# Exchanging the halves of each weight chunk that VectorE and GpSimd turn into low parts

## The chip, the cores and the metric

The kernel runs on one core of a Trainium2 chip. The metric is the device time of one execution in microseconds (us), as the median of several runs. Engines are named as in the profile: PE is TensorE, PEld its weight loads, DVE is VectorE, ACT is ScalarE, POOL is GpSimd, SP is SyncE, which issues the loads of weights.

## The reference, cut to what matters

Two transformer-like blocks follow each other on 256 tokens (272 with 16 extra ones in the first block), with a model width of 1024, all in float32.

```
block 1: n = rmsnorm(h); z = n @ w_in          -> q, k, v, glu, two gates
         differential attention, causal depthwise conv (31 taps), gates
         h += m @ w_out
         up = conv3(rmsnorm(h) @ w_up); h += (silu(gate) * val) @ w_down     (hidden width 2816)
         h = rmsnorm(h)
block 2: z = rmsnorm(h) @ w_in_2               -> rope attention, HGRN2 recurrence, gates
         h += mixed @ w_out_2
         cross attention to 256 memory tokens (wq_x, wkv_x, wo_x)
         h += (silu(a) * b) @ w_down, with a, b = rmsnorm(h) @ w_up
out = rmsnorm(h)
```

The change touches none of these formulas. It concerns how the weight matrices are prepared for the matmuls.

## The kernel before

**Weights as chunks.** All weight matrices are laid out as 166 chunks of 128 partitions x 2048 columns (1 MB), in the order in which they are used. SP loads them into the slots of a ring in SBUF. One chunk gives two output tiles of 128 channels (eight blocks of 128 rows each, 24 matmuls a tile when the chunk is split).

**Split products.** Most phases keep float32 precision by splitting. A value is rounded to a high part (type fp32r), and the low part is the value minus the high part. A product is then three passes of fast matmuls: high weight x high input, high weight x low input, low weight x high input. So PE needs a chunk's high part when it begins the chunk, and its low part only for the third pass of its first tile (`wait_low`, which waits for both halves).

**Who makes the parts.** ACT makes the high part in two copies of 1024 columns, the columns of half 1 first and those of half 0 second (line L997). `split_high` counts these copies. The low part is made by `low_half` (L404), one subtraction of 128 x 1024 for each half:

```
def high_parts(phase, i, c, free):        # ScalarE, L997
    ...
    for half in (1, 0):
        cols = slice(half * HALF_CHUNK, (half + 1) * HALF_CHUNK)
        sc.activation(parts[:, p, cols], ring[:, slot, cols], ACT.Copy).then_inc(split_high, 1)

def low_half(eng, phase, i, c, half):     # L404
    ...
    eng.wait_ge(split_high, STREAM.split(phase, i, c) * 2 - half)
    eng.tensor_tensor(parts[:, LOW - HIGH + p, cols], ring[:, slot, cols], parts[:, p, cols].bitcast(F32), ALU.subtract)\
       .then_inc(split_low[half], 1)
```

So the wait of half 1 is met after the first copy, and that of half 0 after the second. Before the change DVE makes half 1 and POOL makes half 0 (`low_v`, `low_g`, and the call in `add_tiles`). In the phases heads1 and mem_v POOL makes both halves itself (`both`); the change leaves them as they are. The DVE halves that are concerned number 112. The parts are double buffered: ACT may write the high part of chunk c+2 when PE has finished chunk c, and SP may reload a ring slot when both halves of the low part are made.

**Order of the work.** Every engine runs a queue written out by hand, and the low halves stand at fixed places in the queues of DVE and POOL. The places that matter are these.

- up1 (the first block's gate and value projections, 5 loop iterations of two groups, and one group at the end, `up1_end`). A group is two chunks, that is four tiles e = 0 to 3. For each tile ACT makes a first tap (L974), DVE adds two taps (L1678, L1679, reading the tile in PSUM and an accumulator in SBUF), and for e = 2, 3 DVE multiplies by the silu of the gate (L1684, two inputs in SBUF). ACT computes the silus after e = 1, and then copies a chunk's high part; it copies the second chunk's after its tap of e = 3. DVE's queue for a group is: taps e0, taps e1, low half, taps e2, L1684, taps e3, L1684, low half. POOL's is: low half, low half, and then the high and low parts of the two hidden tiles (L2011, L2015).
- down1: nothing but chunks of the down projection, with one low half a chunk on each engine. DVE has the tables for rope in between (`tables1`, L1705 to L1729), then low halves again.
- heads2 (4 iterations, 8 chunks each): attention and the recurrence run beside the projections. POOL makes differences for the decays (L2081, L2082), ACT their exponentials (L1264), DVE the products `level` (L1769, L1771, two inputs in SBUF), and PE the products of these (L818, L828). Low halves stand in between.
- up2 and down2: as up1 and down1, without taps. DVE scales a tile by the norm (L1962, L1969) and multiplies by the silu (L1971).

Of the kernel before, what the change touches and what calls it, by code (L numbers as in the profile page):

```python
# [222 lines left out]
def blocks_kernel(nc, a):  # L223
    ctx = ExitStack()
    with ctx:
# [56 lines left out]
        def col(name, j=0, n=1):  # L282
            return table[:, AT[name] + j:AT[name] + j + n] if isinstance(j, int) else \
                table[:, bass.ds(j + AT[name], n)]
# [107 lines left out]
        def splits_between(phase, then):  # L392

            if phase in SPLIT:
                return [(phase, 2, 2, 3), (phase, 3, 4, 5), (then, 0, 6, 7), (then, 1, 8, 8)]
            return [(then, 0, 4, 5), (then, 1, 6, 7)] if then else []

        def low_half(eng, phase, i, c, half):

            slot, p = STREAM.at[phase][5][c % len(STREAM.at[phase][5])], STREAM.parity(phase, c)  # L400
# [5 lines that stand above are left out]
# [1042 lines left out]
        def _(ve):  # L1448
# [167 lines left out]
            def add_tiles(phase, dst, width, then=None, raw=None, low=None, weight=None, which=None):  # L1616

                def low_raw(t):
                    ve.wait_ge(x_high_ready, INPUTS[which] * KB + t + 1)
                    ve.scalar_tensor_tensor(low[:, t, 0:SEQ], dst(t), col(weight, t), raw[:, t, 0:SEQ].bitcast(F32),  # L1620
                                            ALU.mult, ALU.subtract).then_inc(x_low_ready, 1)

                for t in range(KB + 1):
                    if raw is not None and t == KB:
                        low_raw(t - 1)
                    for name, c, _, at in splits_between(phase, then):
                        if t == at:
                            low_half(ve, name, 0, c, 1)
                    if t < KB:
                        b = STREAM.bank(phase, t)  # L1630
                        ve.wait_ge(tile_done, STREAM.done(phase, 0, t))
                        ve.scalar_tensor_tensor(dst(t), ps[:, b, 0:width], HALF[phase], dst(t), ALU.mult, ALU.add)\  # L1632
                          .then_inc(tile_read[b], 1)
                    if raw is not None and 0 < t < KB:
                        low_raw(t - 1)
# [5 lines left out]

            HALF = {"mix_out1": 0.5, "mix_out2": 0.5, "cross_out": 1.0}
            def low_v(phase, i, c):
                low_half(ve, phase, i, c, 1)

            def down_low(down, between=None):
                for d in range(2, 8):
                    low_v(down, d // 4, d % 4)
                    if between and d == 3:
                        between()  # L1650
                for d in range(3):
                    low_v(down + "_end", 0, d)

            add_tiles("mix_out1", lambda t: res[:, t, Q0:T1], TQ, "up1")
            norm(TQ, lambda k: res[:, k, Q0:T1], lambda k: sq[:, k, 0:TQ], "norm_ffn_w", 3)
            x_low_parts(x_low, sq, x_high, TQ, "ffn1")

            def behind(phase, i, c, up):

                if phase == up:  # L1660
                    low_v(up, i, c + 2)
                else:
                    low_v("down" + up[-1], 0, c)
# [250 lines left out]
            for t in range(KB):  # L1914
# [8 lines left out]
                if t in (5, 7):  # L1923
                    low_v("mix_out2", 0, (t - 5) // 2)
            low_mixed(7)
            add_tiles("mix_out2", lambda t: res2[:, t, :], SEQ, "cross_q", cross_high, cross_low, "norm_x_g_2", "cross")
            inverse_root(SEQ, 6)
            n.next(bank_full[4], 3)
# [12 lines left out]
            for h in range(4):  # L1941
# [9 lines left out]
                if h < 2:  # L1951
                    query_x(h + 2)
            add_tiles("cross_out", lambda t: res2[:, t, :], SEQ, "up2", x_high, x_low, "norm_ffn_g_2", "ffn2")
            inverse_root(SEQ, 7)

# [32 lines left out]
        def _(gp):  # L1988
# [1 line left out]
            n = Tally("gpsimd")  # L1990

            def low_g(phase, i, c):
                low_half(gp, phase, i, c, 0)

            def add_squares(which, first, end, width):

# [21 lines left out]
            def ffn_parts(up, down, made, width):  # L2018

                add_squares("ffn" + up[-1], 1, 5, width)  # L2020
                low_g(up, 0, 0)
                add_squares("ffn" + up[-1], 5, 7, width)
                low_g(up, 0, 1)
                with gp.Fori(0, 5) as i:
                    n.enter(up, i)
                    for g in range(2):
                        low_g(up, i, 2 * g + 2)
                        low_g(up, i, 2 * g + 3)
                        made(up, i, g)
                        hidden_parts(i * 4 + 2 * g)  # L2030
                    n.leave(5)
                low_g(down, 0, 0)
                low_g(down, 0, 1)
                low_g(down, 0, 2)
                made(up + "_end", 0, 0)
                hidden_parts(20)
                for d in range(3, 8):
                    low_g(down, d // 4, d % 4)
                for d in range(3):
                    low_g(down + "_end", 0, d)  # L2040
# [151 lines left out]
```

## Time and profile before

| what | value |
| --- | --- |
| time, median of 3 runs | 1288.91 us (1288.39 to 1289.3) |
| the profiled execution: its own time | 1288.91 us |
| the profiled execution: span of the core | 1287.1 us |
| mean granted TensorE clock | 0.968 of full speed |
| PE busy | 1192.1 us, 93% |
| DVE busy | 701.5 us, 55% |
| ACT busy | 572.4 us, 44% |
| POOL busy | 570.1 us, 44% |

The times of rows are microseconds from the start of the span. A busy share is a mean over very different stages; what counts for a change is which engine's work ends last in the stage that it touches. "Idle before" in a row is the time that the engine had nothing to run ahead of it, with the instruction that ended the wait.

### The profile page before, as it was taken

The numbers are of one execution on the slowest core, as the hardware profiler recorded it, in microseconds if no ns is written. First come the engines' busy times: TensorE is split into PE (matmuls) and PEld (weight loads), VectorE is DVE, ScalarE is ACT, GpSimd is POOL, SyncE is SP. The second block draws the span as 40 slices with busy tenths as digits, with TensorE's granted clock in tenths as the row PEclk, the third lists the DMA queues.
The fourth block names the chain that finished last, engine by engine and source line by source line (L and its number), as shares of the span: only waits on it lengthen the run. The fifth ranks groups of instructions, "written<-read, shape, count | busy, mean of one in ns | idle before, by whom it ended". The sixth has DMA issues, their size and how long they took to land.

```text
span 1287.1 us, 24300 instructions
## 1 busy us (share of the span) xinstructions
PE 1192.1 (93%) x8716; PEld 1122.9 (87%) x8716; DVE 701.5 (55%) x1318; ACT 572.4 (44%) x1074; POOL 570.1 (44%) x407
## 2 busy tenths in 40 slices
PE   4899999988989999997789989998989989999996
PEld 3899999987879999997778879897869979999996
DVE  4362846579436777627664665656364714444323
ACT  4444544434035665445535355453513534444332
POOL 1566666651034666532443435344201603665641
PEclk9999999988999999998899899999989999999999
DMA  5443444433323455541332413233225405545530
GB/s 233 138 158 131 145 149 145 148 135 131 132 98 128 167 180 179 194 166 66 132 113 89 159 65 130 98 130 130 98 98 196 164 34 196 178 181 193 183 148 34
DMA packets 26008, 179.32 MB, mean 139 GB/s; under 512 B 2784, under 2 KB 3936, under 8 KB 4448
## 3 DMA queue, kind: packets, MB, share of 16 engines
q1 hardware_dynamic: 25520, 176.24, 38.1%
q10 hardware_dynamic: 432, 2.31, 0.5%
q8 instruction: 38, 0.62, 0.2%
q14 instruction: 18, 0.15, 0.0%
HBM read 177.49 MB, written 1.05 MB: 139 GB/s over the span
## 4 chain that ended last, share of the span: by engine, by line
PE 77%; DVE 11%; issue 6%; ACT 3%; POOL 2%; DMA 1%; DVEq 0%; ACTq 0%; POOLq 0%; SPq 0%
PE ps L527 44%; PE ps L470 10%; PE ps L753 8%; PE ps L818 2%; PE ps L495 2%; POOL parts L404 1%; PE ps L595 1%; PE ps L567 1%; PE ps L783 1%; DVE branch L1684 1%; PE ps L811 1%; DMA res<-h_in 1%; PE ps L623 1%; DVE rinv L1459 1%; ACT parts L997 1%
## 5 line engine op out<-in xcount | busy, mean ns | idle before, releaser
L404 POOL TENSOR_TENSOR parts<-ring,parts 128x1024 fp32r<-128x1024 f32 x184 | 453.2, 2472 | 538.2 <-ACT parts L997 538.1
L527 PE MATMUL ps<-x_high,parts 128*128 128x256 f32 (+2 forms) x3072 | 418.3, 285 | 9.9 <-DVE x_low L1467 4.3
L527 PEld LDWEIGHTS ps<-x_high,parts 128*128 128x128 f32 x3072 | 387.8, 190 | 21.3 <-issue 7.8
L997 ACT ACTIVATE parts<-ring 128x1024 fp32r<-128x1024 f32 x296 | 295.8, 1049 | 116.2 <-PE ps L753 64.7
L527 PE MATMUL ps<-x_low,parts 128*128 128x256 f32 (+2 forms) x1536 | 218.9, 285 | 0.0
L404 DVE TENSOR_TENSOR parts<-ring,parts 128x1024 fp32r<-128x1024 f32 x112 | 143.4, 1281 | 122.1 <-ACT parts L997 122.0
L527 PEld LDWEIGHTS ps<-x_low,parts 128*128 128x128 f32 x1536 | 200.7, 191 | 0.0
L1538 DVE SCALAR_TENSOR_TENSOR ps<-glu,table_sb,ps 128x256 f32<-128x256 f32 x232 | 93.4, 479 | 0.0
L753 PE MATMUL ps<-act_high,parts 128*128 128x256 f32 x704 | 86.9, 279 | 0.3 <-DVE parts L404 0.3
L753 PEld LDWEIGHTS ps<-act_high,parts 128*128 128x128 f32 x704 | 84.6, 188 | 0.5 <-issue 0.5
L2001 POOL TENSOR_TENSOR sq<-sq 128x256 f32<-128x256 f32 (+1 forms) x18 | 17.2, 956 | 130.9 <-ACT sq L974 130.7
L527 PE MATMUL ps<-parts,x_high 128*128 128x256 f32 x448 | 65.8, 295 | 6.7 <-DVE work L1835 6.7
L527 PEld LDWEIGHTS ps<-parts,x_high 128*128 128x128 f32 x448 | 59.3, 197 | 10.4 <-issue 10.4
L983 ACT ACTIVATE work<-ps 128x256 f32<-128x256 f32 (+2 forms) x52 | 20.0, 386 | 99.5 <-PE ps L527 99.5
L974 ACT ACTIVATE sq<-res 128x256 f32<-128x256 f32 (+2 forms) x56 | 20.9, 412 | 91.0 <-DVE res L1632 74.4
L470 PE MATMUL ps<-branch,ring 128*128 128x256 f32 x256 | 56.0, 379 | 0.7 <-ACT branch L1402 0.7
L470 PEld LDWEIGHTS ps<-branch,ring 128*128 128x128 f32 x256 | 48.5, 190 | 7.9 <-ACT branch L1402 1.4
L1493 DVE MEMSET ps<- 64x128 f32 x16 | 2.6, 165 | 83.1 <-PE ps L623 83.1
L753 PE MATMUL ps<-act_low,parts 128*128 128x256 f32 x352 | 45.5, 282 | 0.0
L753 PEld LDWEIGHTS ps<-act_low,parts 128*128 128x128 f32 x352 | 43.4, 189 | 0.0
L1769 DVE TENSOR_TENSOR res<-glu,sq 128x128 f32<-128x128 f32 x56 | 39.6, 707 | 5.1 <-ACT sq L1264 3.0
L974 ACT ACTIVATE work<-work 128x256 f32<-128x256 f32 x44 | 18.3, 418 | 49.0 <-DVE work L1962 33.0
(263 smaller groups left out, 1594.7 us busy)
## 6 DMA issues: line engine op xcount, KB each, us to landing
ring<-weights SPq DMA_DIRECT2D x166, 1024.0 KB, 4.8
table_sb<-table ACTq DMA_DIRECT2D x1, 1102.0 KB, 6.1
res<-h_in SPq DMA_DIRECT2D x4, 272.0 KB, 8.7
act<-mem ACTq DMA_DIRECT2D x1, 1024.0 KB, 8.8
out<-xT SPq DMA_DIRECT2D x1, 1024.0 KB, 4.7
work<-positions ACTq DMA_DIRECT2D x1, 128.0 KB, 3.1
```

Source lines behind the costliest of these rows:

```text
L404: eng.tensor_tensor(parts[:, LOW - HIGH + p, cols], ring[:, slot, cols], parts[:, p, cols].bitcast(F32), ALU.subtract)\
L470: mm = pe.matmul(ps[:, b, 0:width], ring[:, slot, k * CW + e * P:k * CW + e * P + P], moving(k), start=k == 0, stop=k == KB - 1)
L495: mm = pe.matmul(ps[:, bank, 0:width], ones, src[:, k, 0:width], start=k == order[0], stop=k == order[-1])
L527: mm = pe.matmul(out, left(k), right(k), start=step_ == 0 and k == 0, stop=step_ == 2 and k == KB - 1)
L753: mm = pe.matmul(ps[:, DOWN_BANK + t // 2, t % 2 * SEQ:(t % 2 + 1) * SEQ], w[:, kk * D + t * P:kk * D + t * P + P], x[:, kb + kk, 0:SEQ], ...
L818: mm = pe.matmul(ps[:, bank, at + HD * blk:at + HD * blk + HD], kl[:, l, blk * P:blk * P + P], ql[:, l, blk * HD:blk * HD + HD], start=Tru ...
L974: ins = sc.activation(out, src, fn, **kw)
L983: sc.activation(out, src, fn, scale=scale).then_inc(tile_read[b], 1)
L997: sc.activation(parts[:, p, cols], ring[:, slot, cols], ACT.Copy).then_inc(split_high, 1)
L1538: ve.scalar_tensor_tensor(acc, u, w, acc, ALU.mult, ALU.add).then_inc(dve_step, 1)
L1769: ve.tensor_tensor(halves(kl[:, l, :], m)[:, :, 0, :], halves(kh[:, i * 2 + h, :], m)[:, :, 0, :], e[:, :, 0, :], ALU.mult)
L2001: ins = gp.tensor_tensor(sq[:, 0, 0:width], sq[:, 0, 0:width], sq[:, k, 0:width], ALU.add)
```

## The change

In `add_tiles`, `low_v` and `low_g` the last argument of `low_half` is exchanged: DVE now makes half 0 and POOL half 1. ACT's order of copies stays (half 1, then half 0). So POOL's wait is met by ACT's first copy, and DVE's by the second.

```diff
@@ add_tiles, vector queue
                     for name, c, _, at in splits_between(phase, then):
                         if t == at:
-                            low_half(ve, name, 0, c, 1)
+                            low_half(ve, name, 0, c, 0)
@@ vector queue
             def low_v(phase, i, c):
-                low_half(ve, phase, i, c, 1)
+                low_half(ve, phase, i, c, 0)
@@ gpsimd queue
             def low_g(phase, i, c):
-                low_half(gp, phase, i, c, 0)
+                low_half(gp, phase, i, c, 1)
```

## Rows read from the trace of the kernel before

**Rows 1.** The page's first part: busy time, share, instructions.

```profile
PE 1192.1 (93%) x8716; PEld 1122.9 (87%) x8716; DVE 701.5 (55%) x1318; ACT 572.4 (44%) x1074; POOL 570.1 (44%) x407
```

**Rows 2.** The waits of PE's weight loads and matmuls: us in total, times, longest.

```profile
PEld ps L527 <- POOL parts L404: 3.4, 6, 1.2
```

**Rows 3.** Line L404 over the whole run: duration min/median/max in ns.

```profile
L404 POOL TENSOR_TENSOR parts<-ring,parts x184: 2347/2449/3695, 26.1 to 1263.0; 128x1024 fp32r<-128x1024 f32 x184
L404 DVE TENSOR_TENSOR parts<-ring,parts x112: 1209/1225/3422, 366.2 to 1262.0; 128x1024 fp32r<-128x1024 f32 x112
```

**Rows 4.** Timeline, DVE, last tap of e1: first and eleventh group of up1.

```profile
392.31 0.49 DVE L1679 SCALAR_TENSOR_TENSOR work<-ps,table_sb,work 128x256 f32<-128x256 f32 x1 [0.15 <-DVE work L1678]
...
509.60 0.48 DVE L1679 SCALAR_TENSOR_TENSOR work<-ps,table_sb,work 128x256 f32<-128x256 f32 x1
```

**Rows 5.** Timeline, DVE, one group of up1: start, us, instruction, idle before.

```profile
439.33 0.48 DVE L1679 SCALAR_TENSOR_TENSOR work<-ps,table_sb,work 128x256 f32<-128x256 f32 x1
441.24 1.23 DVE L404 TENSOR_TENSOR parts<-ring,parts 128x1024 fp32r<-128x1024 f32 x1 [1.43 <-ACT parts L997]
442.78 0.48 DVE L1678 SCALAR_TENSOR_TENSOR work<-ps,table_sb,work 128x256 f32<-128x256 f32 x1 [0.31 <-ACT work L974]
...
444.04 0.99 DVE L1684 TENSOR_TENSOR branch<-work 128x256 f32 x1
444.95 0.47 DVE L1678 SCALAR_TENSOR_TENSOR work<-ps,table_sb,work 128x256 f32<-128x256 f32 x1
...
446.28 1.87 DVE L1684 TENSOR_TENSOR branch<-work 128x256 f32 x1 [0.23 <-DVE work L1679]
448.08 1.21 DVE L404 TENSOR_TENSOR parts<-ring,parts 128x1024 fp32r<-128x1024 f32 x1
...
450.85 0.48 DVE L1679 SCALAR_TENSOR_TENSOR work<-ps,table_sb,work 128x256 f32<-128x256 f32 x1
```

**Rows 6.** Timeline, ACT, POOL and PE in the same group.

```profile
440.17 2.00 ACT L997 ACTIVATE parts<-ring 128x1024 fp32r<-128x1024 f32 x2
...
443.39 2.00 ACT L997 ACTIVATE parts<-ring 128x1024 fp32r<-128x1024 f32 x2
...
442.24 2.50 POOL L404 TENSOR_TENSOR parts<-ring,parts 128x1024 fp32r<-128x1024 f32 x1 [2.58 <-ACT parts L997]
445.47 2.41 POOL L404 TENSOR_TENSOR parts<-ring,parts 128x1024 fp32r<-128x1024 f32 x1 [0.72 <-ACT parts L997]
...
444.80 2.19 PE L527 MATMUL ps<-x_high,parts 128*128 128x258 f32 x16 [0.19 <-POOL parts L404]
```

**Rows 7.** Timeline, ahead of cross_q: DVE's half requested while POOL's runs.

```profile
1002.92 2.66 POOL L404 TENSOR_TENSOR parts<-ring,parts 128x1024 fp32r<-128x1024 f32 x1
...
1003.24 3.42 DVE L404 TENSOR_TENSOR parts<-ring,parts 128x1024 fp32r<-128x1024 f32 x1
```

**Rows 8.** Timeline of down1, behind the tables.

```profile
537.38 1.99 ACT L997 ACTIVATE parts<-ring 128x1024 fp32r<-128x1024 f32 x2
...
538.56 4.57 DVE L404 TENSOR_TENSOR parts<-ring,parts 128x1024 fp32r<-128x1024 f32 x2
...
539.93 0.83 PE L753 MATMUL ps<-act_high,parts 128*128 128x256 f32 x5 [0.30 <-DVE parts L404]
```

**Rows 9.** Timeline of heads2, second iteration.

```profile
744.87 2.48 POOL L404 TENSOR_TENSOR parts<-ring,parts 128x1024 fp32r<-128x1024 f32 x1 [12.63 <-ACT parts L997]
745.26 2.24 DVE L1769 TENSOR_TENSOR res<-glu,sq 128x128 f32<-128x128 f32 x1 [0.15 <-ACT sq L1264]
...
747.31 0.45 POOL L2081 TENSOR_TENSOR sq<-conv 128x128 f32 x1
...
748.78 0.49 PE L828 MATMUL ps<-work,act 128*128 128x128 f32 x2 [1.08 <-DVE sq L1771]
```

**Rows 10.** Timeline, DVE, one group of up2.

```profile
1108.58 1.22 DVE L404 TENSOR_TENSOR parts<-ring,parts 128x1024 fp32r<-128x1024 f32 x1
...
...
1113.16 0.42 DVE L1962 TENSOR_TENSOR work<-ps,rinv 128x256 f32<-128x256 f32 x1 [2.42 <-PE ps L527]
```

## The prediction, made before the kernel after was seen

> **What bounds the kernel now.** I read the page's busy shares first, then PE's waits, then line L404 (the low halves), then the timelines of the stages in which low halves stand. PE is busy 93% of the span and no other engine more than 55% [rows 1], so the change can gain only what PE waits for low halves, and loses only where it makes PE wait. PE's weight loads waited for POOL's low half 6 times, 3.4 us in all [rows 2]; that is the whole gain to be had from low parts that come earlier. POOL needs 2.45 us for a half and DVE 1.22 us [rows 3], and DVE starts first. The change gives the first start to the slow engine, which on paper ends the pair 1.0 us sooner.
>
> **Do the two engines' halves run side by side?** This decides everything, and the trace says no. In up1 ACT's two copies start at 440.17 and end at 442.17 [rows 6]. DVE's half starts at 441.24 and ends at 442.47 [rows 5]; POOL's starts at 442.24 and ends at 444.74 [rows 6], which is 2.27 us after DVE's end. Where POOL is alone a half takes 2.41 us (445.47) [rows 6]. The other way round POOL's half ran from 1002.92 to 1005.58, DVE's was issued at 1003.24 and ended at 1006.66: 3.42 us instead of 1.22, and 1.08 us after POOL's end [rows 7]. The same shows in DVE's L1684, which reads two inputs in SBUF: issued at 444.04 it ended at 445.03, 0.29 us behind POOL's half, and issued at 446.28 it ended at 448.15, 0.27 us behind POOL's end at 447.88 [rows 5, 6]. DVE's taps L1678, which read PSUM and one input in SBUF, keep their 0.47 to 0.48 us beside POOL's half (442.78) [rows 5]. So an operation of DVE with two SBUF inputs and one of POOL exclude each other, and whoever holds the memory finishes first.
>
> **The change part by part.** Say ACT's first copy of a chunk is visible at 0.
>
> Before: DVE 0 to 1.23, POOL 1.0 to 1.23 + 2.27 = 3.50. After: POOL 0 to 2.41, DVE issued at 1.0, done at 2.41 + 1.08 = 3.49. The low part is ready at the same time, so PE gains nothing. But DVE leaves at 3.49 instead of 1.23, 2.26 us later, and what stands behind the half in its queue waits. POOL leaves 1.1 us earlier; its next work is either another half, which waits for ACT, or a short operation that must then let DVE's half pass. The only question left is where DVE has 2.26 us to spare.
>
> *up2, and the down stages without tables.* DVE's last low half of a group starts at 1108.58, and would end at 1108.58 + 2.41 + 1.08 = 1112.07; one scaling of 0.42 us follows, done by about 1112.5, and the next, at 1113.16, waits for PE, with 2.42 us idle before it [rows 10]. The delay goes into that idle time: 0. In the down stages DVE has only low halves to make: 0. If this cover were absent, 11 groups of up2 would cost as those of up1, below.
>
> *up1.* Here DVE has almost no idle time. Let T be the end of the last tap of e1, 439.33 + 0.48 = 439.81 [rows 5]. The next T is 450.85 + 0.48 = 451.33, 11.52 us later, and DVE's only idle pieces of note between them are 1.43 us ahead of the first half and 0.31 and 0.23 us later [rows 5]. Over ten groups the mean is (510.08 - 392.80) / 10 = 11.73 us [rows 4]. After the change, relative to T:
> - ACT's copies start at T+0.36 as now (they follow the silu of e1) and the first is visible at T+1.43. POOL's half T+1.43 to 3.84. DVE's half is done at 3.84 + 1.08 = 4.92, against T+2.66 now.
> - Taps e2 start at 4.84; their L1684 follows 1.26 us after the first tap's start, as now (442.78 to 444.04) [rows 5], at T+6.10.
> - ACT's second pair starts at T+3.58 (443.39) [rows 6], its first copy is visible at T+4.66. POOL is free, but DVE's half holds the memory until 4.92, so POOL's second half ends at 4.92 + 2.27 = 7.19. L1684 is blocked until then and ends at 7.47.
> - Taps e3 start at 7.39; L1684 follows 1.33 us after (444.95 to 446.28), at 8.72. POOL is idle, so it costs not 1.87 us but 0.34 to the next instruction (the 0.42 us of 256 columns, as L1962 in rows 10, less an overlap of 0.08) [rows 10]. The second low half runs from 9.06.
> - From there to the next T it takes what it takes now: 451.33 - 448.08 = 3.25 us. T' = 9.06 + 3.25 = T+12.31.
>
> PE does not hide this: the next T needs DVE itself, ACT's copies follow T, and PE starts a chunk when the copies are there. A group goes from 11.73 to 12.31 us, +0.58, times ten: **+5.8 us**. Bounds: below, 0, if the second L1684 and the order of the pieces give back all of it; above, the whole 2.26 us in every group would be 22.6 us, less the one block of L1684 that goes away (1.87 - 0.34 = 1.5 us a group), so 7.6 us, and a second block of 1 us in half the groups would make it 12.6. I take the walk through the queue.
>
> The Trainium skill, in "SBUF — State Buffer", section "Who interferes with whom", says that the pair of ports that DVE and GpSimd share is an exclusive lock, held for a whole instruction, and that the second one to issue fully blocks. By that a blocked half would need its whole 1.22 us after POOL's end, not the 1.08 of the trace, and a blocked L1684 its 0.42, not 0.28. Each group would be 0.28 us longer and the sum 2.8 us larger. I stay with the rows.
>
> *down1, behind the tables.* PE already waits 0.30 us at 539.93 for DVE's half [rows 8], issued at 538.56 when all its inputs are long there. ACT's next copies start at 537.38, so the first is visible at about 538.45 to 538.50. Now POOL waits for the second; after, its half is released some 0.06 to 0.1 us ahead of DVE's and takes the memory until about 538.5 + 2.41 = 540.9. DVE's is then done at 542.0 instead of 539.8: **+2.1 us** on PE, once. Both times hang on the same activation of ACT, so the margin should hold; bounds 0 (DVE wins the race) and 2.3. I take 2.1.
>
> *heads2.* DVE's `level` products read two SBUF inputs, so they already wait for POOL: the first behind the half, issued at 745.26, ends at 747.50, 0.15 us behind POOL's half at 747.35 [rows 9]. After, POOL's half starts 1.0 us sooner, at 743.87, and ends at 746.3, and DVE's ends at 747.4: the products start 0 to 0.1 us later than they end now. One of POOL's waiting differences (0.45 us, 747.31) [rows 9] can slip in ahead, so I take +0.4 us. PE waits for these products (748.78, 1.08 us idle) [rows 9]. The other seven low halves of an iteration come out of the same walk through the timeline with no time on PE: behind them DVE either has a product that waits for POOL already, or idles until PE or ACT is ready. 4 x 0.4 = **+1.6 us**, bounds 0 and 4 x 2.3 = 9.2 (if a half of POOL gets in front of a product of level 5, as in the third rival).
>
> *add_tiles* at the ends of mix_out1 and cross_out: both copies are done when DVE comes to its half, nothing changes. At cross_q the delays end in DVE's waits for PE: 0, bounds -1 and +1.
>
> Sum: 5.8 + 2.1 + 1.6 = 9.5 us. The profiled execution took 1288.91 us, which is also the median, so 1288.91 + 9.5 = **1298.4 us**.
>
> **The rivals.**
> 1. *The low parts come sooner and PE's waits vanish.* If POOL's half did not block DVE's, the pair would be ready at POOL's end, T+3.84 instead of 4.93, and the 3.4 us of rows 2 would go: 1285.5 us. It decides if DVE's half, issued 1 us behind POOL's, still takes 1.2 us. Rows 7 speak against it; for it speaks only that the usual order in this trace is the reverse.
> 2. *Nothing to be measured.* DVE is 55% busy, and if up1's queue gives back the 2.26 us (a block of L1684 that goes, as above, but twice a group) and DVE wins the race in down1: 1288.9 to 1291 us. For it: up2 and down do hide it. Against: up1's idle pieces of 0.31 and 0.23 us.
> 3. *Much slower through heads2.* POOL's half, now released by the first copy, gets the memory just ahead of the last product that PE waits for; each such case costs up to 2.3 us, 4 iterations up to 9 us more: 1307 us. By my estimate the product starts only 0.1 to 0.2 us ahead of POOL's release, which small delays ahead of it could eat.
>
> **How the numbers follow.** My forecast (1293 to 1303 us): 0.68. Rival 1: 0.08. Rival 2: 0.12. Rival 3: 0.12. The predicted time is the forecast's own, 1298.4. The range leaves out rival 1 and rival 3 and takes in most of rival 2 and of the forecast: 1289 to 1304 us. About 0.2%, 2.6 us, is what a measurement of this kernel can tell from no change; faster by more 0.07, within 0.11, slower by more 0.82.
>
> **What would show it.** Many DVE rows of L404 at about 2.5 us (issued 1 us behind POOL's) instead of 1.22, and POOL's median falling from 2.45 to about 2.4; the distance from T to T in up1 at 12.3 us; in down1 one PE wait of about 2.4 us for DVE's low half; up2's matmuls without gaps, as now. The prediction is wrong if DVE's halves stay at 1.22 us, if the group of up1 stays at 11.7 us, or if the iterations of heads2 grow by over a microsecond each.

## The result, and the profile after

The changed kernel takes 1295.77 us (median of 6 runs, 1294.27 to 1298.69) against 1287.56 us (6 runs, 1286.41 to 1289.3) in the same session: 1.0064 times as long, 95% interval 1.0050 to 1.0079, or 8.2 us more. The forecast was 1298.4 us, 9.5 us more. The profiled execution took 1295.04 us, its span 1293.1 us.

The page's first part, to be held against [rows 1]:

```profile
PE 1190.6 (92%) x8716; PEld 1119.8 (87%) x8716; DVE 775.6 (60%) x1318; ACT 572.1 (44%) x1074; POOL 599.2 (46%) x407
```

The number of instructions is the same on every engine, and DVE is busy 74.1 us longer (775.6 - 701.5). That is no new work: the time that a half stands blocked behind POOL's counts as busy, as the next rows show. Line L404 over the whole run, as in [rows 3], duration min/median/max in ns:

```profile
L404 POOL TENSOR_TENSOR parts<-ring,parts x184: 2341/2402/4604, 25.1 to 1268.0; 128x1024 fp32r<-128x1024 f32 x184
L404 DVE TENSOR_TENSOR parts<-ring,parts x112: 1210/2575/3405, 366.1 to 1268.9; 128x1024 fp32r<-128x1024 f32 x112
```

DVE's median half went from 1225 to 2575 ns, POOL's from 2449 to 2402. The two first figures of the prediction's list are there: DVE's halves are now issued while POOL's run and end behind them. This is so in 89 of the 112 halves of DVE, and each of the 89 ends 1.08 or 1.09 us after the POOL half that it stood behind; in the kernel before, 89 halves of POOL end 2.20 to 2.27 us after DVE's.

The waits of PE's matmuls (not of its weight loads, as in [rows 2]) for low parts, first before, then after:

```profile
PE ps L527 <- POOL parts L404: 2.0, 6, 0.9
```

```profile
PE ps L527 <- DVE parts L404: 4.2, 10, 0.4
PE ps L753 <- DVE parts L404: 2.6, 1, 2.6
PE ps L527 <- POOL parts L404: 1.8, 2, 0.9
```

The waits for low parts were not removed. DVE's half has become the one that ends last in ten groups (0.4 us each), and one wait of 2.6 us stands in down1. The waits for POOL that are left stand at 31.2 and 47.1 us, in a stage where POOL makes both halves. One of the six of [rows 2], of 1.2 us at 32.2 us, is of this kind too: of the 3.4 us that rival 1 wanted to win, the change could touch 2.1 at most.

DVE's timeline in one group of up1, to be held against [rows 5], and POOL's in the same group, against [rows 6]:

```profile
440.87 0.49 DVE L1679 SCALAR_TENSOR_TENSOR work<-ps,table_sb,work 128x256 f32<-128x256 f32 x1
443.74 2.58 DVE L404 TENSOR_TENSOR parts<-ring,parts 128x1024 fp32r<-128x1024 f32 x1 [2.38 <-ACT parts L997]
...
447.49 1.36 DVE L1684 TENSOR_TENSOR branch<-work 128x256 f32 x1
...
450.11 0.43 DVE L1684 TENSOR_TENSOR branch<-work 128x256 f32 x1 [0.23 <-DVE work L1679]
450.45 1.22 DVE L404 TENSOR_TENSOR parts<-ring,parts 128x1024 fp32r<-128x1024 f32 x1
...
453.23 0.48 DVE L1679 SCALAR_TENSOR_TENSOR work<-ps,table_sb,work 128x256 f32<-128x256 f32 x1
```

```profile
442.84 2.40 POOL L404 TENSOR_TENSOR parts<-ring,parts 128x1024 fp32r<-128x1024 f32 x1 [1.62 <-ACT parts L997]
445.71 2.86 POOL L404 TENSOR_TENSOR parts<-ring,parts 128x1024 fp32r<-128x1024 f32 x1 [0.47 <-ACT parts L997]
```

T, the end of the last tap of e1, is 440.87 + 0.49 = 441.36. The walk of the prediction can be read off, with its own number in brackets: POOL's half ends at T+3.88 (3.84), DVE's at T+4.96 (4.92), the first L1684 is issued at T+6.13 (6.10), POOL's second half ends at T+7.21 (7.19), the first L1684 at T+7.49 (7.47), the second is issued at T+8.75 (8.72) and takes 0.43 us instead of 1.87, the second low half starts at T+9.09 (9.06), and the next T comes at 453.71, T+12.35 (12.31).

PE waits for DVE's half once in this group. Its blocks of 24 matmuls (two rows each, the first of them shown) start 2.88 us apart where nothing is missing, which makes 11.52 us for the four of a group:

```profile
442.75 2.23 PE L527 MATMUL ps<-x_high,parts 128*128 128x258 f32 x16
...
446.38 2.19 PE L527 MATMUL ps<-x_high,parts 128*128 128x258 f32 x16 [0.43 <-DVE parts L404]
...
449.37 2.07 PE L527 MATMUL ps<-x_high,parts 128*128 128x258 f32 x16
```

With the wait they start 3.63 and 2.99 us apart, so a wait that the profile puts at 0.43 us costs the group 0.86. In the kernel before, every second group has a wait of 0.19 us for POOL's half ([rows 6], at 444.80), which costs it 0.47 by the same count. So the sum of PE's waits is less than what the stage loses.

PE's matmuls in down1, after and then before (the last of [rows 8], whole), and for the kernel after the granted clock (PEclk) ahead of and behind the wait:

```profile
547.15 5.57 PE L753 MATMUL ps<-act_high,parts 128*128 128x256 f32 x32 [2.63 <-DVE parts L404]
```

```profile
539.93 4.01 PE L753 MATMUL ps<-act_high,parts 128*128 128x256 f32 x32 [0.30 <-DVE parts L404]
```

```profile
core 0: us, PE busy (x) PEld busy (x) DVE busy (x) ACT busy (x) POOL busy (x), PEclk, DMA share, GB/s
538.00:547.10 9.10, 6.52 (x56) 6.31 (x54) 7.10 (x16) 4.23 (x6) 3.08 (x2) 1.00 0.03 12
547.10:555.00 7.90, 7.85 (x53) 7.86 (x54) 3.70 (x2) 2.01 (x2) 2.39 (x1) 0.78 0.70 264
```

The wait was 0.30 us and is 2.63. It is followed by a stretch in which the clock was granted at 0.78 on average, that is partly at 1.2 GHz, and 32 matmuls took 5.57 us. The same 32 matmuls took 4.01 us before, all of that stretch at 1.00. POOL's half of one chunk starts 0.05 us ahead of DVE's half of the chunk before it (0.06 to 0.1 had been forecast):

```profile
543.65 2.36 POOL L404 TENSOR_TENSOR parts<-ring,parts 128x1024 fp32r<-128x1024 f32 x1 [4.93 <-ACT parts L997]
543.70 4.52 DVE L404 TENSOR_TENSOR parts<-ring,parts 128x1024 fp32r<-128x1024 f32 x2
```

**Where the 8.2 us are.** Three profiles each of the kernel before and of the one after (runs before, before_2 and before_3; after, after_2 and after_3, below) were cut at the same instructions of PE. Times in us:

| stretch | before, 3 profiles | after, 3 profiles | difference of means |
| --- | --- | --- | --- |
| all ahead of up1 | 381.40, 380.49, 381.80 | 381.28, 381.92, 381.55 | +0.35 |
| up1 | 131.62, 130.80, 130.80 | 136.61, 136.52, 136.56 | +5.5 |
| down1 | 63.75, 63.75, 63.76 | 67.65, 67.68, 67.65 | +3.9 |
| norm, to the first matmul of forget | 15.90, 15.78, 15.77 | 15.90, 15.90, 15.89 | +0.1 |
| forget and heads2 up to the end of up2 | 616.86, 617.00, 617.01 | 614.12, 614.22, 614.16 | -2.8 |
| down2 and the end | 77.57, 77.58, 77.56 | 77.54, 77.56, 77.61 | 0.0 |
| span | 1287.1, 1285.4, 1286.7 | 1293.1, 1293.8, 1293.4 | +7.0 |

So up1 and down1 lose 9.4 us, and the long stretch from forget and heads2 to up2 gives 2.8 us back.

### The profile page after: what moved, and what is told of

Its sections match the earlier page's. It is cut to its first block, busy times and chain, and to the rows that moved or that the text cites. A ratio compares the mean times of both kernels' runs of the same rounds, so it can differ in the third digit from the quotient of the medians.

```text
span 1293.1 us, 24300 instructions
## 1 busy us (share of the span) xinstructions
PE 1190.6 (92%) x8716; PEld 1119.8 (87%) x8716; DVE 775.6 (60%) x1318; ACT 572.1 (44%) x1074; POOL 599.2 (46%) x407
## 4 chain that ended last, share of the span: by engine, by line
PE 75%; DVE 12%; issue 7%; ACT 4%; DVEq 1%; DMA 1%; POOL 0%; ACTq 0%; SPq 0%
PE ps L527 41%; PE ps L470 11%; PE ps L753 9%; PE ps L818 2%; PE ps L495 2%; ACT parts L997 2%; PE ps L595 2%; DVE work L1678 1%; DVE work L1679 1%; PE ps L567 1%; DVE rinv L1459 1%; DVE parts L404 1%; PE ps L811 1%; PE ps L623 1%; DMA res<-h_in 1%
## 5 line engine op out<-in xcount | busy, mean ns | idle before, releaser
L404 POOL TENSOR_TENSOR parts<-ring,parts 128x1024 fp32r<-128x1024 f32 x184 | 448.4, 2447 | 491.5 <-ACT parts L997 491.5
L404 DVE TENSOR_TENSOR parts<-ring,parts 128x1024 fp32r<-128x1024 f32 x112 | 258.9, 2313 | 160.4 <-ACT parts L997 160.3
L2081 POOL TENSOR_TENSOR sq<-conv 128x128 f32 x56 | 45.9, 820 | 16.0 <-ACT sq L1264 15.5
L2011 POOL CAST act_high<-branch (+1 forms) x44 | 36.2, 850 | 21.6 <-DVE branch L1684 21.6
```

The costliest lines, as they stand in the source:

```text
L2011: gp.tensor_copy(act_high[:, j + x, :], branch[:, j + x, 0:SEQ]).then_inc(hidden_high, 1)
L2081: gp.tensor_tensor(d[:, :, 0, :], middle, b[:, :, 0, :], ALU.subtract)
```

## The experiments

### Does the start of the slow engine matter, or which columns it has?

mirror is the changed kernel, with ACT's copies turned round too, so that DVE's half is again the one whose copy comes first. The columns stay as in the changed kernel.

```diff
-                for half in (1, 0):
+                for half in (0, 1):
@@ low_half
-            eng.wait_ge(split_high, STREAM.split(phase, i, c) * 2 - half)
+            eng.wait_ge(split_high, STREAM.split(phase, i, c) * 2 - (1 - half))
```

> The kernel after, with ACT's two copies in the other order (half 0 first) and the waits to match, so DVE again has the half that is ready first and POOL the second. If only the order of the two engines matters: the time of the kernel before (ratio to it 1.000, within 0.2%), DVE's halves at 1.22 us, POOL's at 2.45 us, T to T in up1 11.7 us on the mean, 0.3 us of PE wait for DVE's half in down1. If it matters which columns an engine gets (addresses), the time stays near the kernel after, 1.006.

Measured: 1289.77 us (11 runs, 1287.27 to 1291.98) against 1288.18 (23 runs), 1.0014 (1.0006 to 1.0023). Line L404 has the durations of before:

```profile
L404 POOL TENSOR_TENSOR parts<-ring,parts x184: 2342/2449/3647, 25.9 to 1263.8; 128x1024 fp32r<-128x1024 f32 x184
L404 DVE TENSOR_TENSOR parts<-ring,parts x112: 1209/1225/3425, 366.3 to 1262.8; 128x1024 fp32r<-128x1024 f32 x112
```

Ten groups of up1 take 510.83 - 393.29 = 117.5 us, as before (117.3), down1 63.69. So nearly all of the loss comes from who is released first, and little or nothing from the columns. A rest of 1.6 us is left, which the interval doesn't take for chance. Part of it is a side effect of the edit. In heads1 and mem_v POOL makes both halves, half 1 first, and with ACT's copies turned round it has to wait for the second copy before it can start. PE's longest wait for it, in mirror and then in before_2:

```profile
47.81 2.14 PE L527 MATMUL ps<-parts,x_high 128*128 128x256 f32 x16 [1.82 <-POOL parts L404]
```

```profile
46.69 2.16 PE L527 MATMUL ps<-parts,x_high 128*128 128x256 f32 x16 [0.88 <-POOL parts L404]
```

That is 0.9 us more; where a profile has this wait without mirror's edit (before_2, before_3, the three of after), it is 0.88 to 0.90 us. The remaining 0.7 us stay open: 32 matmuls (L595) at the head of up1 took 6.82 us in mirror's profile, but as they took 6.41 in before, 5.62 in before_2 and 5.63 after, one profile can't tell this from chance.

### Is the loss in up1, and how much of it?

up1_only makes the exchange in up1 and up1_end alone, not_up1 everywhere else.

```diff
+FLIP = ("up1", "up1_end")     # not_up1: all other phases
-        def low_half(eng, phase, i, c, half):
+        def low_half(eng, phase, i, c, half, by=None):
-               .then_inc(split_low[half], 1)
+               .then_inc(split_low[half if by is None else by], 1)
@@ vector queue
+                low_half(ve, phase, i, c, 0 if phase in FLIP else 1, 1)
@@ gpsimd queue
+                low_half(gp, phase, i, c, 1 if phase in FLIP else 0, 0)
```

The last argument `by` only keeps each engine on its own counter of finished halves, whichever half it makes; the call in `add_tiles` is edited like the one in the vector queue.

> The change in the phases up1 and up1_end alone. By my sum this is the largest part: T to T 12.36 us as in the kernel after against 11.73, ten groups, so +6 us or a ratio of 1.0045 to 1.005; down1 and heads2 as before. The rival, that the time comes from the down stage and from heads2 and that up1's loss is taken up later by slack, would give 1.000 to 1.001 here.

> The change everywhere but in up1 and up1_end. My sum as corrected by the trace after: +2.3 us and about 1.3 us of slower matmuls behind it in down1, -1.8 us in heads2, -1.4 us behind heads2: about 0 to +2 us, a ratio of 1.000 to 1.0015. If heads2's shorter time after was chance, +3.5 us, 1.0027.

| kernel | us (runs) | ratio, interval | up1 | down1 | heads2 to up2 |
| --- | --- | --- | --- | --- | --- |
| up1_only | 1293.04 (5) | 1.0042 (1.0029 to 1.0055) | 136.56 | 63.75 | 616.88 |
| not_up1 | 1290.38 (11) | 1.0022 (1.0013 to 1.0031) | 131.55 | 67.73 | 614.18 |

The parts add up: +4.9 and +2.2 make 7.1 us of the 8.2, within the intervals. Both missed the range that was expected by a little: up1_only came out under its 1.0045 to 1.005, not_up1 above its 1.000 to 1.0015. up1 alone holds more than half of the loss, and each stage shows the time of the change only where the change is in it. not_up1 is the sum of two opposite things: down1 +4.0 and the stretch from heads2 to up2 -2.8.

### Which of the two halves of a group costs?

up1_first makes the exchange only for the first low half of a group of up1, up1_second only for the second.

```diff
+def flipped(phase, i, c):
+    return phase == "up1" and c % 2 == 0     # up1_second: c % 2 == 1
@@ vector queue
+                low_half(ve, phase, i, c, 0 if flipped(phase, i, c) else 1, 1)
@@ gpsimd queue
+                low_half(gp, phase, i, c, 1 if flipped(phase, i, c) else 0, 0)
```

> The exchange in up1 for the first low half of each group of two chunks alone (up1_end included); everything else as before. All is computed. Theory (queue walk with exclusion, relative to T, the end of the last tap of e1): POOL's half T+1.43 to 3.84, DVE's ends at T+4.92, L1684 behind the taps of e2 is issued at T+6.10. POOL's second half now waits for ACT's second copy, starts only at about T+5.7 and ends at about T+8.0, so L1684 is blocked until about T+8.3 (2.2 us instead of 1.36), the second L1684 starts at about T+9.6, and the next T comes at about T+13.1: a group takes about 13.1 us against 11.7 before and 12.36 with both exchanged. Ten groups: about +14 us, ratio to before about 1.011. Rival (each exchanged half costs its own delay, the two adding up to the 0.6 us of a group): a group of 11.9 to 12.1 us, +2 to +4 us, ratio 1.002 to 1.003. Rival 2 (only the first half's delay counts, the second is free): 12.36 us a group, as with both exchanged, ratio 1.004.

> The exchange in up1 for the second low half of each group alone; everything else as before. All is computed. Theory (queue walk with exclusion): DVE's first half ends at T+2.66 as before, the taps of e2 start at about T+3.0, L1684 is issued at T+4.23 and is blocked by POOL's first half until about T+5.2; POOL's second half, released by ACT's first copy, follows at once until about T+7.3, the second L1684 (issued at about T+6.5) is blocked until about T+7.6, and DVE's second half starts at about T+7.5 against T+8.27 before. The next T comes at T+10.8 by DVE's queue, so PE or ACT set it instead: 11.5 to 11.7 us a group, 0 to -2 us in all, ratio 0.998 to 1.000. So the whole of up1's loss belongs to the first half. Rival (the delays add up): 12.0 us a group or more, +3 us or more, ratio 1.002 or above.

Measured: up1_first 1295.78 us (5 runs, 1293.98 to 1297.64), 1.0055 (1.0041 to 1.0069); up1_second 1285.45 us (11 runs, 1284.36 to 1288.92), 0.9986 (0.9977 to 0.9995), against 1288.25 (27 runs). Ten groups of up1, from first to eleventh T:

| kernel | first T | eleventh T | per group |
| --- | --- | --- | --- |
| before | 392.80 | 510.08 | 11.73 |
| before_2 | 391.09 | 508.31 | 11.72 |
| after | 391.90 | 515.30 | 12.34 |
| after_2 | 392.49 | 515.85 | 12.34 |
| up1_first | 391.17 | 518.89 | 12.77 |
| up1_second | 392.72 | 507.19 | 11.45 |

DVE's and POOL's timelines in one group of up1_first (line numbers are 4 higher; the first tap shown ends at T = 416.96):

```profile
416.48 0.48 DVE L1683 SCALAR_TENSOR_TENSOR work<-ps,table_sb,work 128x256 f32<-128x256 f32 x1
419.35 2.58 DVE L408 TENSOR_TENSOR parts<-ring,parts 128x1024 fp32r<-128x1024 f32 x1 [2.38 <-ACT parts L1001]
...
423.09 1.78 DVE L1688 TENSOR_TENSOR branch<-work 128x256 f32 x1
...
426.13 0.43 DVE L1688 TENSOR_TENSOR branch<-work 128x256 f32 x1 [0.23 <-DVE work L1683]
426.47 1.22 DVE L408 TENSOR_TENSOR parts<-ring,parts 128x1024 fp32r<-128x1024 f32 x1
```

```profile
418.45 2.39 POOL L408 TENSOR_TENSOR parts<-ring,parts 128x1024 fp32r<-128x1024 f32 x1 [1.63 <-ACT parts L1001]
422.19 2.39 POOL L408 TENSOR_TENSOR parts<-ring,parts 128x1024 fp32r<-128x1024 f32 x1 [1.35 <-ACT parts L1001]
```

And of up1_second, where DVE's first half is again early:

```profile
428.37 1.23 DVE L408 TENSOR_TENSOR parts<-ring,parts 128x1024 fp32r<-128x1024 f32 x1 [1.43 <-ACT parts L1001]
...
431.17 0.97 DVE L1688 TENSOR_TENSOR branch<-work 128x256 f32 x1
...
433.40 1.72 DVE L1688 TENSOR_TENSOR branch<-work 128x256 f32 x1 [0.23 <-DVE work L1683]
435.04 1.21 DVE L408 TENSOR_TENSOR parts<-ring,parts 128x1024 fp32r<-128x1024 f32 x1
```

The signs came out as the walk said, and both rivals of up1_first fell. The sizes were less exact. For up1_first 13.1 us a group and a ratio of 1.011 had been expected, and 12.77 us and 1.0055 were measured. I had let POOL's second half end at T+8.0, with ACT's second pair of copies as late as before; it ended at 422.19 + 2.39 = 424.58, T+7.6, and L1688 behind it at T+7.9 instead of T+8.3. From there all followed 0.4 us sooner. The timed runs show less than the trace: their median is 7.5 us above before, while the profiled execution, the slowest of the five, has a span of 1295.8 us, 9.4 above the mean of before. By the intervals alone (1.0041 to 1.0069, and 1.0029 to 1.0055 for up1_only) the two kernels could be equally fast; that exchanging the first half alone costs more than exchanging both rests on the ten groups of each trace, which hardly vary.

In up1_second the first half is where it was and the second wins: POOL's second half is released by the first copy, so the second L1688 takes 1.72 us in all, where in the kernel before it took 1.87 in one group of an iteration [rows 5] and 2.35 in the other (434.28 to 436.63). In the place shown groups come every 11.52 us, and PE's matmuls follow each other without a gap: PE is the bound there. Of the two theories for up1_second the walk's came true, a small gain; that the delays add up did not. Its gain over the whole run, 2.8 us, is not all from up1: that stage is 2.1 us shorter than the mean of before, and the norm behind down1 takes 14.21 us instead of 15.8 to 15.9, at a granted clock of 1.00 where before has 0.85 and before_2 0.89, though nothing was changed there.

The exchange of the first half costs 10.4 us over ten groups, that of the second gains 2.8, and both together cost 6.1, not 7.6. What an exchanged half costs depends on where the other pieces of the queue stand, so it can't be priced half by half and summed.

### Is down1's loss the one race, and is the slow clock its doing?

all_but_one is the changed kernel, but for one chunk of down1: the one that POOL is released for just as DVE comes back from the tables to the chunk ahead of it. There POOL keeps half 0, and so waits for the second copy.

```diff
+def flipped(phase, i, c):
+    return (phase, c) != ("down1", 1) or isinstance(i, int) and i == 0
```

> The whole change except in one chunk, the second chunk of down1's second pair behind the tables or wherever the single PE wait of 2.63 us stood: there POOL keeps half 0 and DVE half 1. All is computed. Theory: POOL is no longer released ahead of DVE's waiting half, so PE's wait of 2.63 us falls to about 0.3 us, and the granted clock of the 32 matmuls behind it (0.78, 5.57 us) goes back to full speed (4.0 us). down1 takes 63.7 to 64.2 us instead of 67.65: -3.9 us against the full change, ratio to before about 1.003. Rival (the wait moves to the neighbouring chunk, since POOL's next half is released as early): down1 stays at 66 to 68 us, ratio 1.006. Rival 2 (the slow clock in down1 has another cause than the wait): the wait goes and 5.57 us stay, -2.3 us.

Measured: 1292.10 us (11 runs, 1290.26 to 1295.88), 1.0025 (1.0016 to 1.0034), 3.7 us under the full change; against the kernel before of the same session it loses 3.9 us where the full change lost 8.2. down1 takes 64.04 us. PE's row and the granted clock at the place:

```profile
546.20 4.01 PE L757 MATMUL ps<-act_high,parts 128*128 128x256 f32 x32 [0.58 <-DVE parts L408]
```

```profile
538.00:546.20 8.20, 7.62 (x66) 7.45 (x64) 6.20 (x16) 4.53 (x7) 2.31 (x2) 1.00 0.16 67
546.20:554.00 7.80, 7.80 (x66) 7.80 (x67) 5.78 (x2) 2.01 (x2) 4.52 (x2) 1.00 0.77 271
```

The wait is 0.58 us instead of 2.63, and the 32 matmuls are back at 4.01 us and a clock of 1.00. Both rivals (the wait moves to a neighbour; the clock falls all the same) fell. This one race costs 3.6 us in down1 (67.65 - 64.04): 2.05 us of waiting and 1.56 us of slow matmuls. not_up1, which keeps the race, has both again (67.73).

### Does heads2 gain by the exchange?

In the first pair of profiles heads2 was 2.2 us shorter after the change, where 1.6 us longer was forecast. heads2_only makes the exchange there alone (the edit of up1_only with `FLIP = ("heads2",)`). Then the kernels before and after were each profiled twice more.

> The exchange in heads2 alone; everything else as before. All is computed. Theory (the gain of 2.2 us of forget and heads2 with the full change comes from the pattern of waits in heads2 itself, through where the granted clock falls): heads2 326.5 us instead of 328.7, granted clock about 0.98 in each iteration, -2.2 us, ratio 0.998. Rival (it came from the different time or clock history with which the stage was entered): 328.7 us, ratio 1.000. Rival 2 (the walk of the prediction, without a move of the clock): +0.4 us an iteration, 330.3 us, ratio 1.001.

> The kernel before once more, for its profile. The part of forget and heads2 took 328.7 to 328.9 us in three kernels whose heads2 is as before, and 326.9 to 327.0 in two others (up1_first, up1_second). Theory (the stage has two courses of the granted clock, and an execution falls into one or the other, whatever the kernel): 328.7 or 326.9 us, not the same in every profile of this one kernel. Rival (the course is fixed by the program and by what it did ahead of the stage): 328.7 us each time, with the granted clock 0.95, 0.98, 0.98 in the second to fourth iteration.

> As before_2, a third profile of the kernel before: by chance theory 328.7 or 326.9 us in forget and heads2, by the rival 328.7.

> The changed kernel once more, for its profile. Theory (two courses of the granted clock by chance): heads2 326.5 us or, in some profiles, some 2 us more, about 329; up2 153.6 or 155.5. Rival (fixed by the program): 326.5 us and 153.6 us again. Either way the group of up1 stays at 12.36 us and PE's wait in down1 at 2.6 us, since these come from the queues.

> As after_2, a third profile of the changed kernel: by the chance theory forget and heads2 326.5 or about 329 us and up2 153.6 or 155.5, by the rival 326.5 and 153.6. up1's group 12.36 us and down1's wait 2.6 us in both.

heads2_only: 1286.68 us (11 runs, 1284.08 to 1288.83), 0.9992 (0.9983 to 1.0001); the stage takes 326.94 us in its profile. The single executions, each beside one of before at 1287.32 us: before_2 1287.30, before_3 1288.62, after_2 1295.72, after_3 1295.28.

| kernel | forget, heads2 | up2 | heads2 to up2 |
| --- | --- | --- | --- |
| before | 328.74 | 153.56 | 616.86 |
| before_2 | 326.86 | 155.58 | 617.00 |
| before_3 | 326.89 | 155.54 | 617.01 |
| mirror | 328.86 | 153.55 | 616.98 |
| up1_only | 328.80 | 153.55 | 616.88 |
| up1_first | 327.03 | 155.56 | 617.12 |
| up1_second | 326.88 | 155.59 | 617.04 |
| after, after_2, after_3 | 326.50 to 326.57 | 153.55 to 153.58 | 614.12 to 614.22 |
| not_up1 | 326.56 | 153.58 | 614.18 |
| heads2_only | 326.94 | 153.55 | 614.48 |
| all_but_one | 326.70 | 155.54 | 617.48 |

My first reading had taken one profile for the kernel. The kernel before itself has two courses: either heads2 is 1.9 us longer or up2 is 2.0 us longer, and the sum is the same to 0.3 us in seven profiles of kernels with the old heads2. The windows of forget and heads2 and of up2's head, in before and then in before_2:

```profile
592.67:921.41 328.74, 301.77 (x2225) 278.05 (x2225) 198.98 (x425) 158.28 (x334) 139.46 (x149) 0.95 0.31 112
...
1056.00:1084.00 28.00, 28.00 (x131) 24.69 (x132) 8.55 (x16) 10.91 (x20) 9.55 (x8) 1.00 0.32 113
```

```profile
590.82:917.68 326.86, 301.00 (x2224) 277.33 (x2225) 199.26 (x425) 158.09 (x334) 139.80 (x149) 0.95 0.31 113
...
1054.00:1082.00 28.00, 28.00 (x126) 24.39 (x126) 8.46 (x15) 9.49 (x18) 9.26 (x8) 0.96 0.32 113
```

In up2 it is the granted clock: 1.00 at its head in one, 0.96 in the other, and PE is busy all the time in both. In heads2 it is the clock only in part: PE is busy 0.8 us longer (301.77 against 301.00) and idle 1.1 us longer (27.0 against 25.9). The idle time is one more wait of L828 for DVE's product L1771: before has it in the first two iterations (1.07 and 1.08 us), before_2 and before_3 in the third alone (1.08 and 1.07).

With the new heads2 five profiles of six have neither cost, 2.5 to 2.8 us less in sum; the sixth, all_but_one, has up2 at 155.5 and gains nothing. That PE's own work was quicker, not its waits shorter, shows in the whole stretch of before_2 and of after_2, the same matmuls at 581.2 and 576.0 us of busy time:

```profile
590.82:1207.82 617.00, 581.20 (x4153) 541.24 (x4153) 334.00 (x630) 271.94 (x514) 251.56 (x233) 0.96 0.37 133
```

```profile
602.02:1216.24 614.22, 576.00 (x4152) 536.96 (x4153) 385.10 (x629) 271.86 (x514) 276.07 (x233) 0.97 0.37 134
```

So PE had 5.2 us less of busy time and 2.4 us more of idle time (38.2 against 35.8). Against the first profile of before (579.96 us busy) it is 4.1 us less and 1.3 us more. The slower queues did cost something, and matmuls that ran at a higher granted clock on the mean (0.97 against 0.96 in these two rows) gave back more. up1's group (12.34 us) and down1's wait (2.63 us) stayed in after_2 and after_3, as expected. Of the two theories neither held as it was put: the stage's time is not fixed by the program (before: 328.7, 326.9, 326.9), and the pure chance theory doesn't explain that the changed kernel came out the same three times. That the exchange in heads2 goes with 2.8 us less is seen in five of six profiles; in the timed runs of heads2_only it is 1.6 us, and the interval reaches to 1.0001. Why the low clock comes in fewer stretches is not settled.

### A version without the exclusion

If the two engines exclude each other, POOL's half takes 2.4 us of memory time for what DVE does in 1.2. dve_both gives DVE both halves, except in heads1 and mem_v. Its edit against the changed kernel:

```diff
@@ add_tiles and low_v
+                low_half(ve, phase, i, c, 1)
                 low_half(ve, phase, i, c, 0)
@@ low_g
-                low_half(gp, phase, i, c, 1)
+                return
```

> DVE makes both halves, POOL none (outside heads1 and mem_v). If DVE and POOL exclude each other, POOL's 2.27 us are only in the way: with the first copy visible at 0 the low part is ready at 2.4 us instead of 3.5, DVE leaves at 2.4. In up1 both blocked L1684 shrink from 0.99 and 1.87 us to 0.42, T to T is that of PE, 11.5 us, against 11.73: -2.3 us. In heads2 the level products behind low half 6 are no longer blocked: -1 us in each iteration that waits there, so 0 to -4 us. Together 1281 to 1286 us, ratio 0.995 to 0.999. If the engines do run side by side, taking POOL's half away gives DVE 1.1 us more for each chunk and frees nothing: up1 at 12.5 us or more a group and a ratio of 1.003 to 1.008.

Measured: 1282.44 us (6 runs, 1279.66 to 1284.63), 0.9955 (0.9943 to 0.9968), faster than both kernels by 5.7 and 13.3 us. Line L404:

```profile
L404 DVE TENSOR_TENSOR parts<-ring,parts x224: 1215/1222/1766, 365.8 to 1257.1; 128x1024 fp32r<-128x1024 f32 x112
L404 POOL TENSOR_TENSOR parts<-ring,parts x72: 2350/2402/3698, 25.9 to 291.2; 128x1024 fp32r<-128x1024 f32 x72
```

The median of DVE's 224 halves is what one takes alone. A low part is there 2 x 1.2 = 2.4 us after its first copy instead of 3.5. up1 takes 129.68 us, down1 63.23, and the stretch from heads2 to up2 613.92; of PE's waits for low parts one is left (0.8 us). Its span of 1281.1 us is 5.3 below the mean of the three of before: 1.4 us of it in up1, 0.5 in down1, 3.0 in the stretch from heads2 to up2. In up1 and down1 the trace shows where it comes from: PE's waits for low parts are gone, and L404 no longer stands in the way of DVE's own work. The 3.0 us are about what the exchange gained in the same stretch, so they may in part be the granted clock; no run separates the two. And one engine alone is not the best in every stage: up1_second, which keeps the division, had up1 at 128.94 us. Taking an engine away made the kernel faster, where two engines that take turns had been thought to work side by side.

## Why the prediction was right, by its steps

**Forecast and result.** +9.5 us was forecast and +8.2 measured (7.0 between the means of three spans). The sign, the order of size and the main place were right. Two terms were off, down1's by 1.8 us one way and heads2's by 4.4 the other, so that the sum came out so close is in part luck. The forecast time lies 2.6 us above the measured one: 1.3 us by this difference, and 1.3 by the starting point, since 1288.91 was the median of three runs and 1287.56 that of six.

**Exclusion: right.** Rival 1 fell. DVE's half ends 1.08 us behind POOL's (443.74 + 2.58 = 446.32, and 442.84 + 2.40 = 445.24), the same 1.08 as in [rows 7]. L1684 ended 0.28 us behind POOL's half (448.85, 448.57), as taken. The Trainium skill's rule in "SBUF — State Buffer", section "Who interferes with whom", that the second one to issue fully blocks, agrees in its direction; in its size the measurement decides. By a full 1.22 and 0.42 us behind POOL's end the group would have been 12.6 us, and 12.7 if POOL's second half, which is itself issued behind DVE's, also took its whole 2.41 (the prediction left that one out); by the rows of the trace 12.31; it is 12.34.

**up1, +5.8 us: right.** The ten groups took 6.1 us more (123.4 against 117.3), the whole stage 5.5 by the means of three profiles. Each stop of the walk that was compared above came within 0.05 us. One that was not on the path did not: ACT's second pair came 0.36 us sooner after T than before (444.58, T+3.22, for the T+3.58 that was taken), which changed nothing because DVE's half held the memory until T+4.96. The bound on PE is in the rows above: 0.86 us a group after, 0.47 in every second group before, +0.62 on the mean. That it had to be a walk, and not a count of blocked instructions, shows in up1_first and up1_second: the same exchange costs 1.0 us a group in one place and gains 0.3 in the other.

**down1, +2.1 us: right in place and kind, too small.** The race went as forecast, in all three profiles, and the wait grew by 2.33 us. The step that was mis-sized is the one that put PE's loss equal to its wait: behind it the 32 matmuls took 1.56 us longer at a granted clock of 0.78. Measured +3.9; all_but_one takes back both together.

**heads2, +1.6 us: its mechanism is there, its sum is not.** The wait behind the first iteration's halves grew from 1.07 to 1.44 us, as the estimate of 0.4 had it; but PE has this wait in two of the four iterations after (the first and the fourth) and in one or two before, so the factor of four was not borne out. PE's row after, and the same in before:

```profile
683.04 0.71 PE L828 MATMUL ps<-work,act 128*128 128x128 f32 x4 [1.44 <-DVE sq L1771]
```

```profile
674.32 0.71 PE L828 MATMUL ps<-work,act 128*128 128x128 f32 x4 [1.07 <-DVE sq L1771]
```

From before_2 to after_2 PE's idle time grew by 2.4 us over the stretch from heads2 to up2. What failed is the silent step that matmuls keep their length when the waits around them move: they took 5.2 us less, and the term came out at -2.8 instead of +1.6. Rival 3 (POOL ahead of a product of level 5) didn't come about.

**up2 and the down stages, 0: right.** DVE's half in up2 takes 2.58 us instead of 1.22, and the idle time ahead of the second scaling, 2.42 us in [rows 10], takes it up and still has 0.72 us:

```profile
1126.92 2.58 DVE L404 TENSOR_TENSOR parts<-ring,parts 128x1024 fp32r<-128x1024 f32 x1 [0.32 <-ACT parts L997]
1129.42 0.41 DVE L1962 TENSOR_TENSOR work<-ps,rinv 128x256 f32<-128x256 f32 x1
1130.56 0.42 DVE L1962 TENSOR_TENSOR work<-ps,rinv 128x256 f32<-128x256 f32 x1 [0.72 <-PE ps L527]
```

up2 was 153.58 us, as in one profile of before (153.56), and down2 63.20 as there. Rival 2 was right for these stages and wrong for up1.

## What to carry to other kernels

Before dividing an elementwise operation between VectorE and GpSimd, look in the trace at one instruction of each that overlap: if the later one ends a fixed time behind the earlier, wherever it was issued, they run in turn. Then the division buys nothing by itself, and the faster engine alone is worth trying (here 0.45% over the whole kernel). When the order of two such operations is turned round, their common end doesn't move, but the wait moves to the engine that now comes second; price it by walking that engine's queue to the next point that other engines need. A wait put on TensorE can cost more than its length, by a slower clock behind it, and one profile of a kernel is not its time in a stage: profile both kernels more than once before explaining 2 us.

## What the runs showed of the hardware that was not expected

- The pair of halves takes the same time in either order: DVE's ends 3.5 us after the first copy with POOL first, and so does POOL's with DVE first. The second one ends 1.08 us (DVE) or 2.25 to 2.27 us (POOL) behind the first, some 0.14 us less than it takes alone.
- The wait of 2.63 us for TensorE in down1 was followed by a granted clock of 0.78 over 7.9 us in the changed kernel, and one of 0.58 us in the same place by a clock of 1.00.
- A wait of 0.43 us of TensorE in up1 delays the matmuls behind it by 0.86 us, counted from start to start.
- Without any change of the program, before took one of two courses: 1.9 us more in heads2 (0.8 of it busy and 1.1 idle time of TensorE), or 2.0 us more in up2, at a lower granted clock.
